# Experts of a mixture layer: the last two k tiles of gate and up walked by halves of the FF channels

## The reference

```python
def expert_block(args):
    x_blk, e = args
    a = x_blk @ w_gate[e]
    u = x_blk @ w_up[e]
    return (jax.nn.silu(a) * u) @ w_down[e]

yb = lax.map(expert_block, (xb, block_e)).reshape(cap, d)
return jnp.zeros((n_tok, d), h.dtype).at[buf_tok].add(buf_w[:, None] * yb)
```

## Time and profile before

| | |
|---|---|
| time, median of 3 runs | 2187.74 us (2185.46 to 2194.51) |
| the profiled execution | 2190.55 us, span of its instructions 2188.8 us |
| busy over the span | PE 94%, PEld 64%, DVE 21%, ACT 15%, POOL 12% |
| expert stage, 1237 to 2131 us | PE busy 875.43 of 894.00 us, granted clock 1.00 |

### The profile page before, as it was taken

One profiled execution on the slowest core, in us unless ns is written; L12 is line 12 of the kernel. 1 busy time (PEld: TensorE's weight loads), 2 busy tenths in 40 slices (PEclk: granted clock), 3 DMA queues, 4 the chain that ended last, 5 costly groups with the idle time before them and its releaser, 6 DMA issues.

```text
span 2188.8 us, 25917 instructions
## 1 busy us (share of the span) xinstructions
PE 2058.3 (94%) x10100; PEld 1411.7 (64%) x10100; DVE 467.4 (21%) x1040; ACT 324.3 (15%) x724; POOL 254.5 (12%) x272
## 2 busy tenths in 40 slices
PE   7999999999999999999998699999999999999990
PEld 3765455755548654467545588887777777777770
DVE  1034322243221442213432300000000000000003
ACT  1021110111101211002101111111111111111103
POOL 2000000000000000000000122122222222212215
PEclk9999999999999999999998699999999999999995
DMA  7212321213222124121112587777777777777868
GB/s 278 78 58 96 126 87 59 77 58 122 110 78 78 56 80 154 59 78 58 59 61 85 218 275 267 264 274 269 267 263 267 266 270 270 269 265 268 276 187 320
DMA packets 71462, 369.13 MB, mean 169 GB/s; under 512 B 8979, under 2 KB 13204, under 8 KB 39520
## 3 DMA queue, kind: packets, MB, share of 16 engines
q1 hardware_dynamic: 49584, 307.39, 38.3%
q0 software_dynamic: 16768, 43.33, 7.9%
q10 hardware_dynamic: 5040, 17.49, 2.0%
HBM read 320.66 MB, written 47.51 MB: 168 GB/s over the span
## 4 chain that ended last, share of the span: by engine, by line
PE 91%; DVE 3%; issue 2%; DMA 2%; ACT 1%; POOL 1%; SPq 0%; POOLq 0%; DVEq 0%; ACTq 0%
PE ps_proj L387 25%; PE ps_proj L552 10%; PE ps_proj L399 9%; PE ps_proj L603 7%; PE ps_proj L605 6%; PE ps_state L619 5%; PE ps_num L619 5%; PE ps_rows L605 3%; PE ps_scores L605 3%; PE ps_scores L603 3%; PE ps_rows L603 3%; PE ps_num L624 3%; PE ps_state L424 1%; DVE kT L1434 1%; DMA hnT<-in_xT 1%
## 5 line engine op out<-in xcount | busy, mean ns | idle before, releaser
L387 PE MATMUL ps_proj<-hnT,ww 128*128 128x512 f32 x1280 | 566.3, 598 | 6.1 <-issue 4.2
L387 PEld LDWEIGHTS ps_proj<-hnT,ww 128*128 128x128 f32 x1280 | 240.3, 192 | 289.5 <-issue 282.1
L399 PE MATMUL ps_proj<-ww,hnT 128*128 128x256 f32 (+1 forms) x1024 | 228.5, 386 | 11.4 <-DVE vx L1187 11.4
L552 PE MATMUL ps_proj<-wo,yT 128*128 128x512 f32 x512 | 224.5, 594 | 4.5 <-DVE yT L1278 4.5
L603 PE MATMUL ps_proj<-hnT,wo 128*128 128x160 f32 x1024 | 227.6, 304 | 0.7 <-ACT hnT L787 0.7
L605 PE MATMUL ps_proj<-hnT,wo 128*128 128x160 f32 x1024 | 223.9, 301 | 0.0
L399 PEld LDWEIGHTS ps_proj<-ww,hnT 128*128 128x128 f32 x1024 | 196.3, 193 | 42.3 <-DVE vx L1187 13.0
L603 PEld LDWEIGHTS ps_proj<-hnT,wo 128*128 128x128 f32 x1024 | 167.1, 191 | 13.9 <-issue 13.9
L552 PEld LDWEIGHTS ps_proj<-wo,yT 128*128 128x128 f32 x512 | 95.8, 190 | 120.0 <-issue 112.2
L605 PEld LDWEIGHTS ps_proj<-hnT,wo 128*128 128x128 f32 x1024 | 167.9, 191 | 0.0
L1434 DVE TENSOR_TENSOR kT<-qT,ps_proj 128x160 f32<-128x160 f32 x64 | 17.7, 318 | 558.0 <-ACT qT L796 558.0
(11 more groups left out here) (254 smaller groups left out, 1873.3 us busy)
## 6 DMA issues: line engine op xcount, KB each, us to landing
wo<-in_w_gu SPq DMA_DIRECT2D x128, 1024.0 KB, 6.3
ww<-in_w_slots SPq DMA_DIRECT2D x52, 1024.0 KB, 4.9
og<-in_w_dn SPq DMA_DIRECT2D x32, 1024.0 KB, 4.8
vx<-in_w_dn SPq DMA_DIRECT2D x32, 1024.0 KB, 7.4
xin<-in_x SPq DMA_DIRECT2D x16, 512.0 KB, 6.0
hnT<-in_xT SPq DMA_DIRECT2D x8, 1024.0 KB, 7.0
xres<-in_x SPq DMA_DIRECT2D x16, 512.0 KB, 4.3
hn_rows<-hn ACTq DMA_DIRECT2D x16, 512.0 KB, 2.7
```

The lines of the kernel that those rows point to most:

```text
L387: mm = pe.matmul(PROJ[:, n % 2, :], slot_weights(slot, k, c, P), hnT[:, k, :], start=(k == 0), stop=(k == KT - 1))
L399: mm = pe.matmul(PROJ[:, n % 2, 0:w], hnT[:, k, t * P:(t + 1) * P], slot_weights(slot, k, 0, w), start=(k == 0), stop=(k == KT - 1))
L552: mm = pe.matmul(PROJ[:, n % 2, :], yT[:, k, t * P:(t + 1) * P], wo[:, k, half * 512:(half + 1) * 512], start=(k == 0), stop=(k == KT - 1))
```

## The change

The walk of `gate_up` over the first six k tiles stays. The last two are walked by halves of the FF channels: k tiles 6 and 7 of m = 0 and 1 first, then k tiles 6 and 7 of m = 2 and 3. A new semaphore `half_done` is counted behind the first half; the fourth `wgu_used` stays behind the last matmul. The first half of `silu` waits for `half_done` and the second for `wgu_used`. `down` waits for one count of `hid_ready` ahead of f = 0 and for the second ahead of f = 2.

```diff
                 pe.wait_ge(S_("xT_ready"), (k + 1) * 3)
                 pe.wait_ge(S_("hid_ready"), k * 2)
-                for kt in range(KT):
-                    if kt % 2 == 0:
+                order_ = [(kt, m) for kt in range(KT - 2) for m in range(FT)]
+                order_ += [(kt, 2 * half + m) for half in range(2) for kt in (KT - 2, KT - 1) for m in range(2)]
+                for n, (kt, m) in enumerate(order_):
+                    if kt % 2 == 0 and m == 0:
                         pe.wait_ge(S_(f"wgu_loaded{kt // 2}"), (k + 1) * 16)
...
+                    if kt < KT - 2 and m == FT - 1 and kt % 2 == 1:
+                        mm.then_inc(S_("wgu_used"), 1)
+                    if kt == KT - 1 and m == 1:
+                        mm.then_inc(S_("half_done"), 1)
+                mm.then_inc(S_("wgu_used"), 1)
 
             def down(k, turned):
 
-                pe.wait_ge(S_("hid_ready"), 2 * (k + 1))
                 for half in range(2):
                     if half == 1:
                         pe.wait_ge(S_("xT_ready"), turned * 3)
                     for f in range(FT):
+                        if half == 0 and f % 2 == 0:
+                            pe.wait_ge(S_("hid_ready"), 2 * k + f // 2 + 1)
                         if half == 0 and f % 2 == 0:
                             pe.wait_ge(S_(f"wd_loaded{f // 2}"), (k + 1) * 16)
...
             def silu(k):
                 for half in range(2):
-                    act.wait_ge(S_("wgu_used"), (k + 1) * NWS)
+                    if half == 0:
+                        act.wait_ge(S_("half_done"), k + 1)
+                    else:
+                        act.wait_ge(S_("wgu_used"), (k + 1) * NWS)
```

More of the change, by code:

```diff
@@ L597, in gate_up @@
                 pe.wait_ge(S_("hid_ready"), k * 2)
-                for kt in range(KT):
-                    if kt % 2 == 0:
+                order_ = [(kt, m) for kt in range(KT - 2) for m in range(FT)]
+                order_ += [(kt, 2 * half + m) for half in range(2) for kt in (KT - 2, KT - 1) for m in range(2)]
+                for n, (kt, m) in enumerate(order_):
+                    if kt % 2 == 0 and m == 0:
                         pe.wait_ge(S_(f"wgu_loaded{kt // 2}"), (k + 1) * 16)
[L601 to L608, removed]
+                    pe.matmul(GU[m][:, 0:CAP], wo[:, kt, m * P:(m + 1) * P], xT[:, kt, :],
+                              start=(kt == 0), stop=(kt == KT - 1), skip_group_check=True)
+                    mm = pe.matmul(GU[m][:, CAP:2 * CAP], wo[:, kt, FF + m * P:FF + (m + 1) * P],
+                                   xT[:, kt, :], start=False, stop=(kt == KT - 1), skip_group_check=True)
+                    if kt < KT - 2 and m == FT - 1 and kt % 2 == 1:
[3 more added lines that the diff above has]
+                mm.then_inc(S_("wgu_used"), 1)
             def down(k, turned):
-                pe.wait_ge(S_("hid_ready"), 2 * (k + 1))
                 for half in range(2):
```

## The result

The changed kernel takes 2164.14 us (median, 2157.65 to 2168.89), the kernel before beside it 2188.32 us. The ratio is 0.9885, with a 95% interval of 0.9861 to 0.9909: 1.15% less time, where 1.2% (2160.5 us) had been forecast. The expert stage can be measured by itself in the two traces, because each item has its transposes at one place. The first is the kernel before, the second the changed kernel (columns as in the earlier trace rows).

The account below looks back on a forecast made before the run. TensorE's stream was taken to bound the expert stage; 31 x 0.82 us plus 1.86 us for the last item gave 27.2 us off the 2187.74 us median, so 2160.5 us, range 2155 to 2171 us.

Parts of the forecast that it names:

- The price of the wait: Expert stage, before `down`'s first load: TensorE's wait for VectorE's product costs 0.82 us per item, at least 0.55 us.
- The last item: Last item, with no transposes to hide silu and product: 1.86 us gained, after a 0.08 us stall ahead of f = 2.
- First half: First silus and products: `hid_ready` counted at 1504.27, wanted by `down` at 1506.10, 1.8 us to spare; 0.7 us in last item.
- Second half: Second silus and products: ready at 1506.45, wanted ahead of f = 2 at 1507.49, 1.0 us to spare.
- The order of the walk and the added count: End of gate and up: reordering the same 16 matmuls and one more semaphore increment per item cost nothing.
- The added wait and register instruction: In `down` ahead of f = 2: costs nothing when the count is there, since f = 2 already waits for `wd_loaded1`.
- The sum: Expert stage: 31 x 0.82 = 25.3 us plus 1.86 us for the last item, 27.2 us gained in all.
- Only the matmul gap: Rival at `down`'s first load: it waits for the transposes' end, so only 18.7 us are gained, 2169 us; chance 0.09.
- the bared load: Rival ahead of f = 2: the added wait exposes a 0.19 us load per item, 21 us gained, 2166.5 us; chance 0.05.
- Transfers as the bound: Rival in the expert stage: 270 GB/s limits weight transfers, period stays 28.22 us, no change, 2186 us; chance 0.06.
- PSUM reads slowing the matmuls: Rival at gate and up's last 2.18 us: ScalarE and VectorE reads slow matmuls, 2230 us if they double; chance 0.04.

Follow-up runs that it names:

- one-tile version: The changed kernel with only the last k tile, not the last two, walked by halves; 2166.71 us, ratio 0.9893 against the kernel before.
- the control: The changed kernel run once more with nothing changed; 2162.42 us, ratio 0.9882 against the kernel before.

## Why the prediction was right

*What bounds the kernel.* TensorE does. No wait of TensorE for another engine is listed in the 30 items, and 22 us more work on ScalarE, in four more silus per item, left them at 822.27 us.

*The price of the wait.* Forecast 0.82 us per item from the loads' beat, 0.55 us as the lower bound from the matmuls' modelled ends. Measured 0.812 us. This choice was the one that mattered: with 0.55 us an item the kernel would have come to 2169 us. `down`'s first load is 0.11 us behind the transposes' last, as in the earlier trace rows. This was reasoned from a row of the mixer and came true as reasoned, so it isn't luck.

*The last item.* Forecast 1.86 us, with a stall of 0.08 us ahead of f = 2 in it. Measured 2.74 - 0.82 = 1.92 us up to `down`'s first load; the stall is 0.05 us of idle time for the load and costs the matmuls nothing.

*The margins.* First half 1.8 us: the one-tile version gave back 1.09 us of it for nothing. Second half 1.0 us: mis-sized, 1.36 us by the versions with more silus, because it was counted up to the load's place on the beat, and a load may miss that by 0.32 us. It carried nothing in the sum but the 0.08 us.

*Edits at no cost.* The order of the walk and the added count: from gate and up's first matmul to the next transposes it's 28.22 - (1515.85 - 1505.12) = 17.49 us before and 27.41 - (1321.27 - 1311.36) = 17.50 us now. The added wait and register instruction: from `down`'s first load to that of its 32-column part, which stands before in the row below, it's 1513.98 - 1506.92 = 7.06 us before and 1319.41 - 1312.34 = 7.07 us now.

```profile
1513.98 0.59 PEld L624 LDWEIGHTS ps_num<-og,kT 128*32 128x32 f32 x16 [0.76 <-issue]
```

*The sum.* 27.2 us forecast, 27.1 us in the two traces' expert stages, 24.2 us in the medians of the result and 27.7 us in those of the control. The 3 us between are within the interval (0.9861 to 0.9909 is 20 to 30 us) and of the size of the scatter ahead of the experts. Two slips did no harm: 31 x 0.82 is 25.4 us, not 25.3; and the first silus were said to start some 2.2 us before the transposes, where the prediction's own places (1503.14 and 1504.98) give the 1.84 us that were measured.

*The rivals.* Only the matmul gap, and the bared load: refuted by the period of 27.41 us and the 7.07 us of `down`. Transfers as the bound: no wait for `wgu_loaded` or `wd_loaded` is listed, at 277 GB/s over 822 us; it was not tried how much more they would bear. PSUM reads slowing the matmuls: line 606's rows in the second half stay 0.27 us a pair apart while ScalarE reads `ps_proj` at 1309.38:

```profile
1309.18 0.43 PE L604 MATMUL ps_scores<-hnT,wo 128*128 128x160 f32 x2
...
1309.45 0.43 PE L606 MATMUL ps_scores<-hnT,wo 128*128 128x160 f32 x2
...
1309.72 0.43 PE L604 MATMUL ps_rows<-hnT,wo 128*128 128x160 f32 x2
```

## What to carry to other kernels

A wait of TensorE is to be priced by the beat of its weight loads, from the last load before it to where the next would stand, not by the idle time between modelled matmul ends: here 0.82 against 0.55 us, and a stall of 0.35 us was in the matmuls' list for none of the 31 items that had it. That holds for a load behind short matmuls, as here behind the transposes; behind matmuls of 512 columns 0.32 us of a load's delay cost nothing. For the same reason a busy share of 100% is no proof that nothing waits. When a consumer takes its input in pieces, split the producer's last work, the epilogue and the consumer's wait together; either alone took 0.46 of 0.81 us here, and half the head start did as well as all of it but for 0.38 us once. Then measure the margin that is left, by adding harmless work until the period moves.

## What was not expected of the hardware

**Spells of half clock behind short gaps, in some executions only.** The mixer before the experts is untouched, yet the transposes of the second item's input come at 1252.01 us in the kernel before, at 1257.41 and 1247.98 in two executions of the changed kernel. The granted clock accounts for most of it. Between 100 and 1180 us, read in windows of half a microsecond, the traces show three short stretches at half clock in the kernel before (10.2 us together), six in the changed kernel's profiled execution (20.5 us) and one in the control (3.4 us). An estimate from that, if half of such time is lost, is 5.1 us more than in the kernel before for the one (5.40 measured) and 3.4 us less for the other (4.03 measured). So the control's expectation, which put three more such stretches at 5 us, agrees with these three executions. At the border between two token blocks TensorE does narrow router matmuls and is then idle for some 1.3 us. In the changed kernel's profiled execution the clock behind that gap is granted at 0.52, which is the 1.2 GHz level for nearly all of the stretch, and in the kernel before at 1.00 (busy time by stretch, the changed kernel first):

```profile
310.20:313.70 3.50, 3.50 (x5) 1.44 (x6) 1.26 (x2) 0.00 (x0) 0.00 (x0) 0.52 0.42 165
```

```profile
310.20:313.70 3.50, 3.50 (x9) 1.53 (x9) 0.54 (x2) 0.00 (x0) 0.00 (x0) 1.00 0.61 242
```

Five matmuls in place of nine were started. The timelines (the changed kernel first again) show that the gap ahead was not longer there, but shorter:

```profile
310.12 6.25 PE L387 MATMUL ps_proj<-hnT,ww 128*128 128x512 f32 x10 [1.29 <-issue]
```

```profile
309.48 6.70 PE L387 MATMUL ps_proj<-hnT,ww 128*128 128x512 f32 x15 [1.38 <-issue]
```

In the control the gap is 1.62 us, and full clock follows it.

The times of the result's and the control's runs follow the mean granted clock of their executions: at 0.979 the kernel before takes 2185.2 and 2185.6 us and the changed one 2157.65 us, at 0.974 to 0.975 they take 2194.4 to 2196.8 us and 2166.5 to 2168.9 us. At like clock the difference is 26 to 30 us, about the forecast; most of the spread of the runs goes with the clock ahead of the experts and not with the edit. Why a spell follows the gap in one execution and not in the next stays open.

**Around the 32-column part the loads stop running ahead.** Between matmuls with 128-column weights a load starts while the matmul ahead runs. Behind the 32-column part the next load has 0.41 us of idle time in front, and the first 32-column load behind 128-column ones 0.76 us, in the changed kernel as before, where 0.24 us are usual. The section "The mechanism" of the Trainium skill's page "TensorE: Matmul & The Clock Gate" ties the overlap, in its list, to different row groups, and in its text also allows it for loads into a background weight buffer. The rows here have the overlap with equal row groups (all loads are of 128 rows) and lose it on either side of the 32-column part.
